# Hybrid decoder trunk, f32: the mixer's input turned plain and scaled by 1/rms after the product, with the projected pieces passing through an SBUF ring and GpSimd

## The reference

```python
def rms_norm(x, w):
    y = xf * lax.rsqrt(jnp.mean(xf * xf, axis=-1, keepdims=True) + EPS)
    return (y * w).astype(x.dtype)
def swiglu(h, w_gate, w_up, w_down):
    return (jax.nn.silu(h @ w_gate) * (h @ w_up)) @ w_down
for l in range(DEPTH):
    h = rms_norm(x, ffn1_norm[l])
    x = x + 0.5 * swiglu(h, ffn1_w_gate[l], ffn1_w_up[l], ffn1_w_down[l])
    h = rms_norm(x, mix_norm[l])
    proj = h @ w_in[l]                  # 1024 -> 3080 columns
    aq, ak, av, pu, dq, dk, dv, dz, db, da = jnp.split(proj, split_at, axis=-1)
    ...                                 # attention (aq ak av), pooling (pu), gated delta rule (the rest)
    yc = gated_deltanet(dq, dk, dv, dz, db, da, dn_conv_w[l], ...)
    x = x + jnp.concatenate([ya, yb, yc], axis=-1) @ w_out[l]
    h = rms_norm(x, ffn2_norm[l])
    x = x + 0.5 * swiglu(h, ffn2_w_gate[l], ffn2_w_up[l], ffn2_w_down[l])
return rms_norm(x, final_norm)
```

## Time and profile before

| | |
|---|---|
| median of 3 runs | 1103.63 us (1102.22 to 1105.7) |
| the profiled execution | 1107.22 us, its span 1105.4 us |
| busy: TensorE, VectorE, ScalarE, GpSimd | 97%, 66%, 55%, 19% |
| granted TensorE clock, mean | 0.992 of full |
| mixer of layer 0, layer 1 | from 207 us and from 746 us |

### The profile page before, as it was taken

How to read it: one execution, slowest core, us unless ns; L and a number is a source line. 1 busy time by engine, 2 the same in 40 slices (tenths; PEclk the granted TensorE clock), 3 DMA queues, 4 the chain that set the end, 5 groups by cost and what they waited for, 6 DMA issues and landing times.

```text
span 1105.4 us, 18284 instructions
## 1 busy us (share of the span) xinstructions
PE 1066.8 (97%) x6179; PEld 929.7 (84%) x6179; DVE 726.8 (66%) x1125; ACT 609.7 (55%) x1057; POOL 213.9 (19%) x255
## 2 busy tenths in 40 slices
PE   6899999899999999999999999998999999999996
PEld 5788888798997788888878888888899878888885
DVE  4666666688437676666677666667773667666665
ACT  5555555567445655555565555556653556555554
POOL 1312112571020131211222112120002002211212
PEclk9899999999999999999999999999999999999999
DMA  6866667364321476666647666674352044766661
GB/s 198 271 186 194 189 183 216 100 168 115 119 73 39 137 240 188 195 188 185 195 133 213 190 183 196 189 202 121 100 152 96 21 152 152 210 189 184 196 191 39
DMA packets 252151, 179.27 MB, mean 162 GB/s; under 512 B 5891, under 2 KB 237576, under 8 KB 251976
## 3 DMA queue, kind: packets, MB, share of 16 engines
q1 hardware_dynamic: 251168, 176.71, 54.3%
q0 software_dynamic: 336, 1.71, 0.4%
q10 hardware_dynamic: 600, 0.22, 0.1%
HBM read 177.57 MB, written 1.05 MB: 162 GB/s over the span
## 4 chain that ended last, share of the span: by engine, by line
PE 87%; DVE 5%; ACT 4%; DMA 2%; issue 1%; POOL 0%; ACTq 0%; DVEq 0%; POOLq 0%; SPq 0%
PE bank L700 27%; PE bank L703 14%; PE bank L666 12%; PE bank L667 11%; PE bank L668 11%; PE bank L985 2%; PE bank L1009 2%; DMA raw<-in_ffn_w_up 1%; DVE Wl L1626 1%; ACT Wh L1215 1%; PE bank L681 1%; DVE X L1672 1%; PE bank L992 1%; ACT big L1248 1%; PE bank L917 1%
## 5 line engine op out<-in xcount | busy, mean ns | idle before, releaser
L1626 DVE TENSOR_TENSOR Wl<-raw,Wh 128x1024 fp32r<-128x1024 f32 x330 | 417.9, 1273 | 131.6 <-ACT Wh L1215 131.3
L1215 ACT ACTIVATE Wh<-raw 128x1024 fp32r<-128x1024 f32 x330 | 337.6, 1053 | 80.6 <-PE bank L668 74.7
L700 PE MATMUL bank<-X,Wh 128*128 128x512 f32 x1344 | 334.8, 391 | 0.0
L700 PEld LDWEIGHTS bank<-X,Wh 128*128 128x128 f32 x1344 | 247.0, 189 | 47.4
L589 POOL TENSOR_TENSOR gact<-gact,pooled 128x256 f32<-128x256 f32 x88 | 77.5, 880 | 606.5 <-DVE gact L1717 464.2
L703 PEld LDWEIGHTS bank<-X,Wl 128*128 128x128 f32 x1344 | 183.2, 191 | 13.8 <-DVE Wl L1626 1.0
L703 PE MATMUL bank<-X,Wl 128*128 128x256 f32 x1344 | 187.8, 283 | 0.0
L666 PE MATMUL bank<-Wh,aH 128*128 128x512 f32 x352 | 140.0, 398 | 6.4 <-DVE aL L1738 6.0
L667 PE MATMUL bank<-Wl,aH 128*128 128x512 f32 x352 | 138.9, 395 | 0.0
L668 PE MATMUL bank<-Wh,aL 128*128 128x512 f32 x352 | 137.9, 392 | 0.0
L1314 ACT ACTIVATE dec<-bank 128x256 f32<-128x256 f32 x88 | 33.6, 382 | 126.1 <-PE bank L703 125.3
(11 more groups left out here) (246 smaller groups left out, 1276.5 us busy)
## 6 DMA issues: line engine op xcount, KB each, us to landing
raw<-in_ffn_w_gate SPq DMA_DIRECT2D x88, 512.0 KB, 4.1
raw<-in_ffn_w_up SPq DMA_DIRECT2D x88, 512.0 KB, 3.7
raw<-in_ffn_w_down SPq DMA_DIRECT2D x88, 512.0 KB, 4.5
raw<-in_w_in SPq DMA_DIRECT2D x50, 512.0 KB, 3.9
raw<-in_w_out SPq DMA_DIRECT2D x16, 512.0 KB, 3.5
cst<-in_consts POOLq DMA_DIRECT2D x1, 1536.0 KB, 9.4
xr<-in_x SPq DMA_DIRECT2D x2, 512.0 KB, 4.5
norm_w<-in_mix_norm SPq DMA_DIRECT2D x2, 512.0 KB, 6.1
```

The costliest lines, as they stand in the source:

```text
L700: nc.tensor.matmul(b[:, :], piece(Wh, s)[:, k, :], X[:, k, :, :], start=k == 0, stop=False)
L1215: return nc.scalar.activation(Wh[:, s, :], raw[:, s, :], ACT.Copy).then_inc(hi_cast.sem, 1)
L1626: return nc.vector.tensor_tensor(Wl[:, s, :], raw[:, s, :], Wh[:, s, :].bitcast(F32), ALU.subtract).then_inc(lo_cast.sem, 1)
```

## The change

The mixer is entered as the FFNs are: plain transposes (`turn_left`, `turn_last`, `enter_mixer`), split with the mixer's norm weight, and products that start block by block. So every projected column lacks 1/rms. For the 16 pieces of q, k, v and z ScalarE copies the bank into one of four ring places in `PM` (`evacuate`), GpSimd multiplies it there by `rB` (`scale`), and `conv_first`, `conv_rest` and `z_silu` read the ring. The gates' copy becomes a multiplication by `rB` on VectorE, and the attention's copies take 1/rms as a scale per row. TensorE now waits for `evacuated` where it waited for `convd` or `z_act`. The weighting of `xr`, the products with `diag` and the split by rows are gone from the mixer, as are two loads of the norm weight; pieces 2 and 3 go to slots 3 and 4 and are cast by ScalarE during the last FFN step.

At the head of the program the rows are turned before the norm weights (which are now three loads), and all squares and 1/rms are made before the first split.

```diff
 # TensorE
+            def enter_mixer(layer):
+                def half(i, j0, wait=False):
...
+                    for j in range(j0, j0 + 4):
+                        k = SPLIT_ORDER[j]
+                        if wait:
+                            block_ready(layer, 1, j)
+                        m = three(bank[i][:, 0:SEQ], piece(Wh, s)[:, k, :], piece(Wl, s)[:, k, :], Xh[:, k, :], Xl[:, k, :],
+                                  j == 0, j == KT - 1)
...
+                pe.wait_ge(*x_new.at(layer, 4 + 3))
+                turn_quarter(1, 0, 1)
+                half(0, 0, True)
+                turn_last(layer, 1)
+                half(1, 0)
+                half(0, 4, True).then_inc(proj.sem, 1)
+                half(1, 4).then_inc(proj.sem, 1)
+                row_root(layer, 1)
 # ScalarE, the mixer's pieces
+                def evacuate(i):
+                    act.wait_ge(*proj.at(layer, i + 1))
+                    if i >= 4:
+                        act.wait_ge(*convd.at(layer, i - 3))
+                    nc.scalar.activation(ring(i), pieces[i][:, 0:SEQ], ACT.Copy).then_inc(evacuated.sem, 1)
...
-                for i in range(8):
+                evacuate(0)
+                evacuate(1)
+                hi_mix(layer, 4)
+                conv_first(0)
+                for i in range(2, 8):
                     hi_mix(layer, i + 3)
-                    conv_first(i)
-                    if i >= 1:
-                        conv_silu(i - 1)
-                        if i % 2 == 0:
-                            square(i // 2 - 1)
+                    evacuate(i)
+                    conv_first(i - 1)
+                    conv_silu(i - 2)
+                    if i % 2 == 1:
+                        square(i // 2 - 1)
                 hi_mix(layer, 11)
+                conv_first(7)
+                conv_silu(6)
+                evacuate(8)
                 conv_silu(7)
+                square(3)
+                hi_mix(layer, 12)
                 conv_first(8)
-                hi_mix(layer, 12)
-                conv_first(9)
-                square(3)
+                evacuate(9)
 # VectorE
-                for i in range(8):
-                    lo_mix(layer, i + 3)
+                lo_mix(layer, 3)
+                take_root(layer, 1)
+                lo_mix(layer, 4)
+                for i in range(6):
+                    lo_mix(layer, i + 5)
                     conv_rest(i)
                 lo_mix(layer, 11)
+                conv_rest(6)
                 dve.wait_ge(*gates_proj.at(layer, 1))
-                nc.vector.tensor_copy(gate_cols, bank[0][:, 0:SEQ]).then_inc(gates_copied.sem, 1)
+                dve.wait_ge(*rb_done.at(layer, 2))
+                nc.vector.tensor_tensor(gate_cols, bank[0][:, 0:SEQ], rB, ALU.mult).then_inc(gates_copied.sem, 1)
+                conv_rest(7)
+                lo_mix(layer, 12)
                 conv_rest(8)
-                lo_mix(layer, 12)
 # GpSimd
-                weigh_rows(layer, 1)
-                if layer == 0:
-                    trig_tables()
-
+                def scale(i):
+                    pool.wait_ge(*evacuated.at(layer, i + 1))
+                    nc.gpsimd.tensor_tensor(ring(i), ring(i), rB, ALU.mult).then_inc(scaled.sem, 1)
+                pool.wait_ge(*rb_done.at(layer, 2))
+                for i in range(11):
+                    scale(i)
                 pool.wait_ge(*gstep.at(layer, 16))
...
+                for i in range(11, 14):
+                    scale(i)
                 for c in range(HALVES):
+                    if c == 1:
+                        scale(14)
+                        scale(15)
                     pool.wait_ge(*lt_raw.at(layer, 2 * c + 2))
...
+                if layer == 0:
+                    trig_tables()
```

More of the change, by code:

```diff
@@ L717, in turn_left, with turn_last, block_ready, row_root @@
                 pe.wait_ge(*x_new.at(layer, 4 * n + 2))
-                turn_quarter(0, 0)
-                turn_quarter(1, 0)
+                turn_quarter(n, 0, 0)
+                turn_quarter(n, 1, 0)
+            def turn_last(layer, n):
+                pe.wait_ge(*x_new.at(layer, 4 * n + 4))
+                turn_quarter(n, 1, 1)
+            def block_ready(layer, n, j):
+                pe.wait_ge(*xl_done.at(layer, 8 * n + j + 1))
+            def row_root(layer, n):
+                pe.wait_ge(*diag_done.at(layer, 2 * n + 2))
+                for c in range(HALVES):
+                    m = nc.tensor.matmul(rbank[n][:, c * P:(c + 1) * P], ones, diag[:, c, :], start=True, stop=True)
+                m.then_inc(rb_ps.sem, 1)
             def first_pair(layer, f, between):
-                T, base = f * TILES, FFN_BASE[f]
+                n, T, base = 2 * f, f * TILES, FFN_BASE[f]
                 def half(b, s, i, wait=False):
@@ L749, in first_pair @@
                 half(ubank[0], 1, 1).then_inc(ups_done.sem, 1)
-                pe.wait_ge(*diag_done.at(layer, 4 * f + 2))
-                for c in range(HALVES):
-                    m = nc.tensor.matmul(bank[0][:, c * P:(c + 1) * P], ones, diag[:, c, :], start=True, stop=True)
-                m.then_inc(rb_ps.sem, 1)
+                row_root(layer, n)
             def enter_ffn(layer, f):
+                n = 2 * f
                 if layer == 0 and f == 0:
+                    pe.wait_ge(consts_in.sem, 16)
                     for c, b in ROW_ORDER:
@@ L1239, in x_ready, with inverse, norm_final, enter @@
                     act.wait_ge(*x_new.at(layer, 4 * n + quarter_no(layer, n, c, b)))
-            def enter_ffn(layer, f, cast=None):
-                n = 2 * f
+            def inverse(layer, n, c):
+                act.wait_ge(*var_done.at(layer, 2 * n + c + 1))
+                nc.scalar.activation(stat[:, c, 3:4], stat[:, c, 2:3], ACT.Ln).then_inc(ln_done.sem, 1)
+                act.wait_ge(*ln_done.at(layer, 2 * n + c + 1))
+                nc.scalar.activation(stat[:, c, 4:5], stat[:, c, 3:4], ACT.Exp, scale=-0.5).then_inc(rs_done.sem, 1)
+            def norm_final():
+                for c in range(HALVES):
+                    for b in range(2):
+                        act.wait_ge(*x_new.at(DEPTH, 2 * c + b + 1))
+                        if c == 1:
+                            act.wait_ge(*ss_done.at(DEPTH, b + 1))
+                        nc.scalar.activation(squares[b], xr[:, c, b * NW:(b + 1) * NW], ACT.Square, scale=D_MODEL ** -0.5,
+                                             accum_out=stat[:, c, b:b + 1]).then_inc(ss_done.sem, 1)
+                    inverse(DEPTH, 0, c)
+            def enter(layer, n):
+                first = layer == 0 and n == 0
                 def square(c, b):
@@ L1253, in split @@
                     if j % 4 >= 2:
-                        act.wait_ge(*xl_done.at(layer, SPLITS[n] + j - 1))
-                    nc.scalar.activation(Xh[:, k, :], xt(k), ACT.Copy,
-                                         scale=nrm_all[:, f, layer, k:k + 1]).then_inc(xh_done.sem, 1)
-                if cast is None:
-                    square(0, 0)
-                    square(1, 0)
-                act.wait_ge(*turned.at(layer, 4 * n + (2 if cast is None else 3)))
-                for j in range(4):
-                    split(j)
-                if cast is None:
+                        act.wait_ge(*xl_done.at(layer, 8 * n + j - 1))
+                    nc.scalar.activation(Xh[:, k, :], xt(n, k), ACT.Copy,
+                                         scale=nrm_all[:, n, layer, k:k + 1]).then_inc(xh_done.sem, 1)
+                square(0, 0)
+                square(1, 0)
+                if first:
                     square(0, 1)
@@ L1268, in enter_ffn @@
                         inverse(layer, n, c)
-                else:
-                    cast(0)
+                    act.wait_ge(zeroed.sem, 2)
+                act.wait_ge(*turned.at(layer, 4 * n + (3 if first else 2)))
+                for j in range(4):
+                    split(j)
+                if first:
+                    hi_first(layer, 0, 0)
+                else:
+                    square(0, 1)
+                    square(1, 1)
+                    for c in range(HALVES):
+                        inverse(layer, n, c)
                 act.wait_ge(*turned.at(layer, 4 * n + 4))
@@ L1802, in conv_rest @@
                 def conv_rest(i):
-                    src = ([bank[b] for b in range(8)] + [bank[1], bank[2], bank[7], bank[0]])[i]
+                    src = ring(i)
                     dst = QK[:, i // 2, i % 2, :] if i < 8 else VT[:, i - 8, :]
```

318 lines of the change are left out of this document (138 added, 180 removed).

## The result

The changed kernel took 1148.3 us (median of 4 runs, 1145.4 to 1150.9) against 1104.7 (4 runs, 1102.2 to 1106.8): a ratio of 1.040, interval 1.036 to 1.043. It is slower, as forecast, but by 43.7 us and not by 24.4, which lies above the forecast range of 1116 to 1138.

A forecast was written before the change was run, and what follows sets the result against it. TensorE, busy 97% of the span, was taken as the bound. Per layer 6.3 + 1.5 + 1.6 + 2.5 + 1.5 = 13.4 us; twice that, less 0.5 and 1.9, gives +24.4, median 1128, range 1116 to 1138.

The forecast's parts named there:

- Entry: Mixer's entry: first product 5.14 us after the last down product, not 12.04; piece 2 starts 4.6 us ahead.
- The ring: q and k loop: casts, convolution and silu wait in a circle, 4.17 or 4.83 us a round; gates 6.3 late.
- a convolution from SBUF may be shorter: Seven convolutions reading SBUF instead of PSUM: at best 0.18 us less a piece; lower bound of the net term -1.3.
- The contention: GpSimd multiplying beside VectorE's convolutions: 0 to 0.54 us a piece, 0.4 taken; net +1.5 a layer (-1.3 to +2.5).
- The gates' chain: After the gates' turn: start 8.0 us later instead of 3.27; of 4.8 extra, 1.6 a layer remain (bounds 1 and 3).
- Clock: Behind the wait at the gates, matmuls at the lower clock: 1.5 us a layer lost (bounds 0 and 2.5).
- The select: `affine_select` behind two GpSimd multiplications delays `DT`'s second half after the last z piece: +2.5 us a layer (2 to 3.3).
- Hidden: `trig_tables` behind the select, start near 285, end near 320, before TensorE asks for the rotation near 336: no cost.
- Head: Program start: squares and roots off the path, first split at about 9.4; 1.9 us saved (1 to 3).
- Every multiplication blocks VectorE fully, in the ring and again behind it: Rival: GpSimd's multiplications block VectorE fully in the q and k loop, again for z and v: 1135; chance 0.15.
- The entry stays as slow as before: Rival: splits at the mixer's entry wait for something new, so 4.6 twice isn't won: 1137; chance 0.03.
- The casts keep ahead: Rival: VectorE takes a convolution before the cast, steps under 2.92 us, entry's gain survives: 1092.5; chance 0.09.

The follow-up runs named there:

- the square alone: Changed kernel with ScalarE's high cast of piece 12, first tap of piece 8 and copy of piece 9 ahead of the fourth square: 1142.9 us, 5.5 less.
- the multiplications behind the ring: Changed kernel without GpSimd's multiplications of the four v and four z pieces (not normalized): 1136.9 us, 11.5 less.
- the opened ring: Changed kernel with each convolution ahead of the same round's low cast in VectorE's q and k loop: 1122.9 us, 25.4 less.
- the last version: Changed kernel with queues reordered, q, k and v multiplied by VectorE in PSUM and two VectorE low casts moved: 1098.7 us, ratio 0.995 to the kernel before.

## Why the direction was right and the size wrong

- *Entry.* Right: 5.08 us for the forecast 5.14. Piece 2 started at 216.22; I had 217.0.
- *The ring.* Right in mechanism and nearly in size: 4.57 and 5.22 a round, where 4.17 and 4.83 were the terms without contention and 0.4 the gross term for it. Wrong was "a convolution from SBUF may be shorter": it takes 1.51 from SBUF too, so neither the 0.18 a piece nor the -1.3 was there. The contention came out near its upper bound (0.49 of 0.54 a convolution), as the rule of the Trainium skill (SBUF — State Buffer, "SBUF: two separate sides") had it. To the gates' turn that makes 9.65 for 7.8: six rounds 1.2 longer than forecast, and a start of the ring 1.0 later.
- *The gates' chain*, "of the 4.8 extra about 1.6 come out", is the step that failed most. With the clock's 1.5 it was 3.1, and 8.98 was measured. The chain started 11.3 us after the gates' turn, not 8.0, because the first piece behind the turn ran at half clock (5.6 us from the turn to the sum of squares instead of 3.1), so the sum of squares came late, and the square, the cast of 12 and convolution 8 with it. TensorE's "some 4 us of other work more than the chain needs" were then used up by VectorE's queue (waits for low casts of 1.68 and 3.60, and 0.28 for GpSimd's table behind the chain; before, one of 0.92). The slack of 4 us had no row behind it, and the term doesn't follow even from it: 4.8 less 4 is 0.8, not 1.6. The runs put prices on it: 5.5 us in both layers for the square alone, 11.5 for the multiplications behind the ring, of which the forecast counted only what the select waits for.
- *Clock.* 1.5 a layer forecast. By the timeline the pieces behind the waits of 6.94 and 3.60 take 5.6 and 4.5 us for 3.1 and 3.0: 4.0 in layer 0. That is read from rows; no run took it apart.
- *The select.* 2.5 forecast, 3.55 measured. The mechanism was half of it: moving the select alone gave nothing, since ScalarE's silus waited for the same multiplications.
- *Hidden.* Right: the trigonometric tables start at 295.27 and end at 328.8, some 10 us later than forecast, and no wait of TensorE names the rotation.
- *Head.* 1.9 forecast, 0.8 timed, which can't be told from nothing; the 0.5 in the trace lies within what traces with the same head differ by. The first split starts at 10.13 and not at 9.4, since VectorE's copy of the norm weights stood behind the roots, and the first down product came at 32.73, as before (32.72). What differs from trace to trace is mostly the clock behind it.
- *Rivals.* "Every multiplication blocks VectorE fully, in the ring and again behind it" (1135) was nearest of those whose mechanism the runs bear out, and held a chance of 0.15. It was true beside the forecast, not in place of it. "The entry stays as slow as before" (1137) is nearer in number, but the entry was as fast as forecast. "The casts keep ahead" was named with the right cause, the order of one convolution and one cast, and is what the opened ring shows, though at 3.02 and not under 2.92 us.
- The range was too narrow at the top because the bounds of the chain (1 to 3) were a feeling for slack, not read from a row.

By the timeline the 8.98 are 4.6 us more waiting and 4.0 of half clock, and 0.4 besides. Open is how much of that waiting the clock itself made. Open too is part of what the last version lacks: of the entries' 9.2 us its two mixers keep 6.9 by the traces (5.7 by the medians), and its TensorE still waits 2.4 us for the mixer's low casts and 1.3 for `DT`.

## What to carry to other kernels

Before pricing a moved instruction, draw the queue of each engine around it and ask whether what it waits for waits, in the same round, for something behind it; swapping two lines then was worth 25 us. When a stall goes through engines that are nearly full, don't count on slack behind it: list what stands in the queues up to the next wait, and add the clock that a wait can take from the next piece. An operation given to a less busy engine is not free if both read the same memory; here the busy engine did it cheaper itself, in PSUM.

## What was not expected of the hardware

- Three fused operations take 1.51 us with the source in SBUF as with it in PSUM (252.09 here). What differs is GpSimd beside them: 1.99 from SBUF, while in the kernel before, with GpSimd busy 26.79 of 29.2 us, a convolution from PSUM stayed at 1.51.
- The blocked operation may be a short one: the first norm of 0.42 us took 2.12 beside GpSimd's 2.08.
- A wait of 2.09 us in the middle of full work was followed by matmuls at 0.50 of the clock in layer 0. The length of the wait alone doesn't decide it: the same wait in layer 1 of the same trace was followed by 1.00, and so was one of 2.10 at this place with the gates' multiplication a round earlier (piece 9 took 2.98 us there):

```profile
802.62 0.39 PE L679 MATMUL bank<-X,Wh 128*128 128x256 f32 x1 [2.09 <-DVE Wl L1664]
```
